# The half swap of a rotary embedding: from a TensorE product to four transfers within SBUF

## The chip, the cores and the metric

The kernel runs on one core of one Trainium2 chip. The metric is the device time of one execution in microseconds (us). TensorE does the matrix products, VectorE and ScalarE the elementwise work, GpSimd a few additions and small loads, and SyncE's queue starts the transfers of the weights. On the profile these are PE (with PEld for its weight loads), DVE, ACT, POOL and SP.

## The reference

Two blocks follow each other on 256 tokens of width 2048, all in float32. The first is a recurrent and banded-attention mixer with a feed-forward part. The second puts 16 learned tokens in front and mixes with two kinds of attention; one of them (heads "a") normalises its queries and keys and then turns them by angles that belong to the token's row and column in a grid:

```
def rope_half(x, ang):
    x1, x2 = jnp.split(x, 2, axis=-1)
    c, s = jnp.cos(ang), jnp.sin(ang)
    return jnp.concatenate([x1 * c - x2 * s, x2 * c + x1 * s], axis=-1)

def axial_rope(x, ang_row, ang_col):
    xr, xc = jnp.split(xf, 2, axis=-1)
    return jnp.concatenate([rope_half(xr, ang_row), rope_half(xc, ang_col)], axis=-1)

    q = axial_rope(rmsnorm(heads_first(qa, A_HEADS, HEAD_DIM), q_g), ang_row, ang_col)
    k = axial_rope(rmsnorm(heads_first(ka, A_KV_HEADS, HEAD_DIM), k_g), ang_row, ang_col)
```

A head has 128 columns: 64 for the row angle and 64 for the column angle, and each 64 are two halves of 32. Turning needs, for every half, the other half of its pair: the "half swap". There are 2 key heads on 272 tokens and 8 query heads on 256.

## The kernel before

**Tiling.** Every weight matrix is read once, in chunks of 256 rows by 512 columns (512 KB). A chunk is loaded by SP into `raw`, rounded to a high part `whi` by ACT (`split_hi`, L899), and the remainder `wlo` is made by DVE (`split_lo`, L1301). TensorE multiplies each chunk in 24 matmuls (`chunk_t`, L446; three products for two halves and four column blocks). There are four slots of `raw`, `whi` and `wlo`. ACT and DVE work four chunks ahead (`LEAD`): at place k, that is behind chunk k, they make the parts of chunk k+4, and ACT's rounding waits until TensorE has finished chunk k (`pe_done`).

**The second mixer.** Its input projection has 13 groups of 8 chunks (`G_IN2`, `NC`), places 0 to 103 by `NC * j + k`. All attention work of this block is done between these chunks, on every engine by a written-out order: behind chunk k, each engine runs what its own list has for place k. No planner is at work; each engine's list is a Python loop, and semaphores join them. Of the list, these matter here:

- `values_turn` (L710 to L712) behind chunks 43 to 47 transposes value tiles, two of them at a place, into PSUM; ACT and DVE copy them out (`values_copy`, DVE L1651 and L1652) and free the PSUM bank for the tile four further on.
- The attention units of heads "b" lie behind chunks 49 to 68: `scores` (L748), `weights_turn` (L771), `values` (L781). `values(u)` writes the one PSUM bank 7 and so waits until DVE has copied unit u-1 out of it (`unit_out`, L1758, semaphore `u_o`), and until ACT has copied the transposed weights (`unit_copy`, L1199, semaphore `u_pt`).
- `b_norm` on DVE and `b_turn` (L802) on TensorE follow at places 70 to 77; at place 78 TensorE waits until ACT (L1220) and DVE (L1780) have copied both turned halves (`bn_copied`) before three transposes at L509.
- The units of heads "a" begin at place 79.

**The rotary step** runs three times, n = 0 (keys, 2 tiles of 272 columns), 1 and 2 (queries, 4 tiles of 256), from places 41, 65 and 74 (`ROPE_FROM`). The raw head is in `qg`. ACT squares it into `qsq` and scales `qg` by the gain (semaphore `nr_ev`, two counts). One place after another then come:

- TensorE, place `first`: `rope_squares`, a product of `qsq` with ones (L722), into a PSUM set.
- ACT, place `first + 1`: `rope_root`, Ln and Exp for the reciprocal root (L1174, L1176), each behind a load of its function table.
- TensorE, place `first + 3`: `rope_turn_halves`, a product of `qg` with the constant `turn` (L732; the swap with its signs), into the same PSUM set.
- DVE, place `first + 4`: `rope` step 0, that product times the sine into `qrot` (L1664), which also frees the PSUM set (`set_free`); then steps 1 to 3 at the places of `ROPE_STEPS`: `qg` times the cosine (L1666), the sum (L1669), times the reciprocal root (L1672).

`turn` is loaded at the start by POOL among eight small constants (`N_CONST`). ACT starts no transfer in this kernel; SP and POOL do. `qg`, `qsq` and `qrot` lie in one large region of SBUF whose tiles stand at fixed distances from its beginning; the region begins behind the named tiles, `turn` among them.

The functions that the change touches:

Of the kernel before, what the change touches and what calls it, by code (L numbers as in the profile page):

```python
# [15 lines left out]
P = 128  # L16
# [64 lines left out]
POS_A = (31, *range(33, 40), *range(41, 48), 49)  # L81

LAMBDA_INIT = 0.8 - 0.6 * math.exp(-0.3 * 0)
N_CONST = 8
N_VEC = 8
VEC_ROWS = 68

# [24 lines left out]
def program(nc, x, w_in, lb_logits, hg_norm_w, rel_bias, w_branch_a, w_branch_b, w_out, norm_mix_w,  # L112
            norm_mlp_w, w_up, w_down, norm_final_w, meta_tokens_2, pre_norm_g_2, w_in_2, q_norm_g_2,
            k_norm_g_2, lambda_q1_2, lambda_k1_2, lambda_q2_2, lambda_k2_2, subln_g_2, w_out_2,
            post_norm_g_2, identity, level_masks, rope_cos, rope_sin, rope_turn, distance, rel_turned, triangles, out):
    with ExitStack() as ctx:
        def sb(name, shape, dt=F32):
            return ctx.enter_context(nc.sbuf_tensor(name, shape, dt))

        def sem(name):  # L120
            return ctx.enter_context(nc.semaphore(name))
# [32 lines left out]
        rs_b, ss_b, rn_b = [b_sums[:, i, :] for i in range(3)]  # L154
        cos_t = sb("cos_t", [P, TM])
        sin_t = sb("sin_t", [P, TM])
        turn = sb("turn", [P, P])
        dist = sb("dist", [P, NT, TM])
        ps = ctx.enter_context(nc.psum_tensor("ps", [P, 8, 512], F32))

        def at(name, kib, shape, dt=F32):
# [124 lines left out]
        br_m, br_hi, br_ready = sem("br_m"), sem("br_hi"), sem("br_ready")  # L286
        up_sq, up_hi, up_ready = [sem(n) for n in ("up_sq", "up_hi", "up_ready")]
        vt_t, vt_c = [sem("vt_t0"), sem("vt_t1")], [sem("vt_c0"), sem("vt_c1")]
        nr_ev, nr_ss, nr_sd, nr_rs, nr_rot, nr_done = [sem(n) for n in (
            "nr_ev", "nr_ss", "nr_sd", "nr_rs", "nr_rot", "nr_done")]  # L290
        u_s, u_nm, u_exp, u_p, u_t, u_pt, u_pv, u_o = [sem(n) for n in (
            "u_s", "u_nm", "u_exp", "u_p", "u_t", "u_pt", "u_pv", "u_o")]
        bn_ss, bn_ms, bn_sd, bn_n, bn_t, bn_y, bn_hi, yb2_ready = [sem(n) for n in (
# [16 lines left out]
        def pset(s):  # L310

            return ps[:, 2 * s:2 * s + 2, :].rearrange("p b (x c) -> p (b x) c", x=2)
# [115 lines left out]
        def _(pe):  # L428
# [293 lines left out]
                    ins = mm(ps[:, 2 * s + i, 0:w], ones[:], src, start=True, stop=True)  # L722
                ins.then_inc(nr_ss, 1)

            def rope_turn_halves(n, s):

                pe.wait_ge(nr_sd, n + 1)
                pe.wait_ge(nr_ev, 2 * n + 2)
                for i in range(2):
                    src = qg[:, i, :] if n == 0 else qg[:, 2 * i:2 * i + 2, 0:T]  # L730
                    w = TM if n == 0 else 2 * T
                    ins = mm(ps[:, 2 * s + i, 0:w], turn[:], src, start=True, stop=True)  # L732
                ins.then_inc(nr_rot, 1)

            def scores(u):
                hd, t = divmod(u % B_UNITS, NT)
                if u == 0:
# [90 lines left out]
            for j in range(G_IN2):  # L828
                c0 = C_IN2 + NC * j
                kv = j < 5  # L830
                if kv:
                    pe.wait_ge(set_free[j % 2], SETS_BEFORE_2 + j // 2)
                    if j == 0:
                        pe.wait_ge(x_ready, 2 * KT + 12)
                    elif j == 1:
                        pe.wait_ge(r_ready, 1)
                    else:
                        pe.wait_ge(kvb_free[j % 2], j // 2)
                    outs = [ps[:, b + i, 0:TM] for b in kv_banks(j) for i in range(2)]
                else:  # L840
                    s = set_of(j)
                    pe.wait_ge(set_free[s], need2[j])
                    outs = blocks(s)
                for k in range(NC):
                    if j == 0:
                        if k == 2:
                            turn_group(2, 3, down_free[3])
                        pe.wait_ge(x_ready, 2 * KT + CK * (k + 1))
                        if k == NC - 1:
                            pe.wait_ge(r_diag, NT)  # L850
                            pe.wait_ge(x_ready, 3 * KT)
                            for t in range(NT):
                                ins = mm(ps[:, 6, t * P:(t + 1) * P], ones[:], diag[:, t, :], start=True, stop=True)
                            ins.then_inc(r_mm, 1)
                    if j == 5:
                        pe.wait_ge(hi_packed, CK * k + CK - 1)
                        pe.wait_ge(lo_packed, CK * k + CK)
                    xh, xl = (None, xw_lo) if kv else (uhi, ulo)
                    chunk_t(c0, k, CK * k, xh, xl, outs, TM if kv else T, k == 0, k == NC - 1, shared=not kv)
                    if j == 5 and k >= 3:  # L860
                        values_turn(2 * (k - 3))
                        values_turn(2 * (k - 3) + 1)
                    for n, first in enumerate(ROPE_FROM):
                        if NC * j + k == first:
                            rope_squares(n, ROPE_SETS[n])
                        if NC * j + k == first + 3:
                            rope_turn_halves(n, ROPE_SETS[n])
                    if j >= J_B:
                        side(NC * (j - J_B) + k)

# [20 lines left out]
        def _(act):  # L891
# [276 lines left out]
            def rope_root(n, s):  # L1168
                act.wait_ge(nr_ss, n + 1)
                if n == 0:  # L1170
                    dst, src = qsq[:, 0:2, :], ps[:, 2 * s:2 * s + 2, 0:TM]
                else:
                    dst, src = qsq[:, :, 0:T], pset(s)
                f(dst, src, ACT.Ln, bias=eps_t[:], scale=1.0 / P).then_inc(nr_sd, 1)  # L1174
                act.wait_ge(nr_sd, n + 1)
                f(dst, dst, ACT.Exp, scale=-0.5).then_inc(nr_rs, 1)  # L1176

            def unit_exp(u):
                act.wait_ge(u_nm, u + 1)
# [48 lines left out]
            for j in range(G_IN2):  # L1228
                for k in range(NC):
# [23 lines left out]
                        side(NC * (j - J_B) + k)  # L1253
                    for n, first in enumerate(ROPE_FROM):
                        if NC * j + k == first + 1:
                            rope_root(n, ROPE_SETS[n])
                    if j == G_IN2 - 1 and k in (1, 3):
                        y_upper(1, k // 2, ob, bn_y, bn_hi)
# [29 lines left out]
        def _(dve):  # L1288
# [362 lines left out]
                nc.vector.tensor_copy(v_nat[:, b, :, :], ps[:, 4 + b % 4, 0:T].rearrange("p (t c) -> p t c", t=2))  # L1651
                nc.vector.tensor_copy(v_meta[0:META, b, :], ps[0:META, 4 + b % 4, T:T + P]).then_inc(vt_c[0], 1)  # L1652

            rope_free = (SETS_BEFORE_2 + 4, need2[7] + 1, need2[8] + 1)

            def rope(n, step):
                s = ROPE_SETS[n]
                w = TM if n == 0 else T
                nb = 2 if n == 0 else 4
                v, r, q = qg[:, 0:nb, 0:w], qrot[:, 0:nb, 0:w], qsq[:, 0:nb, 0:w]  # L1660
                if step == 0:
                    dve.wait_ge(nr_rot, n + 1)
                    src = ps[:, 2 * s:2 * s + 2, 0:TM] if n == 0 else pset(s)
                    tt(r, src, spread(sin_t[:], [0, nb], [1, w]), ALU.mult).then_inc(set_free[s], 1)  # L1664
                if step == 1:
                    own(tt(v, v, spread(cos_t[:], [0, nb], [1, w]), ALU.mult))  # L1666
                if step == 2:
                    dve.wait_ge(set_free[s], rope_free[n])
                    own(tt(v, v, r, ALU.add))  # L1669
                if step == 3:  # L1670
                    dve.wait_ge(nr_rs, n + 1)
# [189 lines left out]
        def _(pool):  # L1861
# [10 lines left out]
            for row, src, n in vectors:  # L1872
# [1 line left out]
            small = [  # L1874
                (lamv[:, 0], row_all(lambda_q1_2, DH)), (lamv[:, 1], row_all(lambda_k1_2, DH)),
                (lamv[:, 2], row_all(lambda_q2_2, DH)), (lamv[:, 3], row_all(lambda_k2_2, DH)),
                (cos_t[:], rope_cos), (sin_t[:], rope_sin), (turn[:], rope_turn),
                (dist[:], distance.rearrange("(t p) k -> p t k", p=P)),
            ]
            assert len(small) == N_CONST  # L1880
# [114 lines left out]
def shape_constants():  # L1995
# [17 lines left out]
    half = np.concatenate([ang[0], ang[0], ang[1], ang[1]], axis=1).T  # L2013
    rope_cos, rope_sin = np.cos(half).astype(f32), np.sin(half).astype(f32)

    turn = np.zeros((P, P), f32)
    for m in range(P):
        if (m // 32) % 2 == 0:
            turn[m + 32, m] = -1.0
        else:  # L2020
            turn[m - 32, m] = 1.0
    qpos = places + META
    kpos = np.concatenate([places + META, np.arange(META)])
    distance = np.abs(qpos[:, None] - kpos[None, :]).astype(f32)
    return {"identity": identity, "level_masks": masks, "rope_cos": rope_cos, "rope_sin": rope_sin,
            "rope_turn": turn, "distance": distance}, {"triangles": triangles}


# [19 lines left out]
```

## Time and profile before

| | us |
|---|---|
| median of 3 runs | 1893.94 |
| the 3 runs | 1893.53, 1894.71, 1893.94 |
| span of the profiled execution | 1893.3 |
| PE busy in it | 1879.6 |
| DVE busy | 1101.4 |
| ACT busy | 889.3 |
| POOL busy | 143.6 |

The span goes from the first to the last instruction of one profiled execution; no other time of that execution is recorded, and the median of the runs stands 0.6 us above its span. Matmuls are pipelined: the start of one to the start of the next tells its cost, not its duration. The granted clock of TensorE is 0.999 over the span.

### The profile page before, as it was taken

The numbers are of one execution on the slowest core, as the hardware profiler recorded it, in microseconds if no ns is written. First come the engines' busy times: TensorE is split into PE (matmuls) and PEld (weight loads), VectorE is DVE, ScalarE is ACT, GpSimd is POOL, SyncE is SP. The second block draws the span as 40 slices with busy tenths as digits, with TensorE's granted clock in tenths as the row PEclk, the third lists the DMA queues.
The fourth block names the chain that finished last, engine by engine and source line by source line (L and its number), as shares of the span: only waits on it lengthen the run. The fifth ranks groups of instructions, "written<-read, shape, count | busy, mean of one in ns | idle before, by whom it ended". The sixth has DMA issues, their size and how long they took to land.

```text
span 1893.3 us, 33876 instructions
## 1 busy us (share of the span) xinstructions
PE 1879.6 (99%) x13432; PEld 1743.7 (92%) x13432; DVE 1101.4 (58%) x1270; ACT 889.3 (47%) x1171; POOL 143.6 (8%) x122
## 2 busy tenths in 40 slices
PE   9999999999999999999999999999999999999998
PEld 9989998999999889988998899899889999899986
DVE  6556766667655555545445445445565556767664
ACT  6544444455544445443444344334454355664543
POOL 2001322411001100000010000000010000000000
PEclk9999999999999999999999999999999999999999
DMA  8566565566565656656665665566556655354454
GB/s 270 184 181 177 181 179 178 165 200 180 168 231 191 214 186 179 194 198 192 196 192 193 194 191 194 194 190 190 189 185 181 179 170 150 105 147 144 156 190 143
DMA packets 176434, 346.47 MB, mean 183 GB/s; under 512 B 10976, under 2 KB 11184, under 8 KB 175776
## 3 DMA queue, kind: packets, MB, share of 16 engines
q1 hardware_dynamic: 174176, 337.76, 57.2%
q0 software_dynamic: 2128, 6.82, 1.4%
q8 instruction: 101, 1.65, 0.4%
q14 instruction: 29, 0.24, 0.0%
HBM read 342.44 MB, written 2.10 MB: 182 GB/s over the span
## 4 chain that ended last, share of the span: by engine, by line
PE 97%; DVE 1%; ACT 0%; DMA 0%; issue 0%; SPq 0%; DVEq 0%; ACTq 0%
PE ps L446 58%; PE ps L458 33%; PE ps L548 1%; PE ps L781 1%; DVE wlo L1301 1%; PE ps L771 1%; PE ps L748 1%; PE ps L791 0%; DMA raw<-in_w_in_dram 0%; ACT whi L899 0%; PE ps L476 0%; PE ps L759 0%; PE ps L599 0%; PE ps L591 0%; DVE xlo L1323 0%; PE ps L610 0%
## 5 line engine op out<-in xcount | busy, mean ns | idle before, releaser
L1301 DVE TENSOR_TENSOR wlo<-raw,whi 128x1024 fp32r<-128x1024 f32 x631 | 796.5, 1268 | 698.1 <-ACT whi L899 697.1
L899 ACT ACTIVATE whi<-raw 128x1024 fp32r<-128x1024 f32 x631 | 664.5, 1058 | 886.3 <-PE ps L446 551.5
L446 PE MATMUL ps<-xhi,whi 128*128 128x256 f32 (+1 forms) x1904 | 542.2, 285 | 0.4 <-DVE wlo L1301 0.3
L446 PE MATMUL ps<-xhi,wlo 128*128 128x256 f32 (+1 forms) x1904 | 531.3, 279 | 0.0
L446 PE MATMUL ps<-xlo,whi 128*128 128x256 f32 x1664 | 462.5, 278 | 0.0
L446 PEld LDWEIGHTS ps<-xhi,whi 128*128 128x128 f32 x1904 | 359.1, 189 | 9.3 <-issue 6.7
L446 PEld LDWEIGHTS ps<-xhi,wlo 128*128 128x128 f32 x1904 | 357.8, 188 | 0.0
L446 PEld LDWEIGHTS ps<-xlo,whi 128*128 128x128 f32 x1664 | 313.4, 188 | 1.5 <-issue 0.7
L446 PE MATMUL ps<-x2hi,whi 128*128 128x256 f32 x1024 | 282.8, 276 | 0.0
L446 PE MATMUL ps<-x2hi,wlo 128*128 128x256 f32 x1024 | 282.7, 276 | 0.0
L446 PE MATMUL ps<-x2lo,whi 128*128 128x256 f32 x1024 | 282.7, 276 | 0.0
L446 PEld LDWEIGHTS ps<-x2lo,whi 128*128 128x128 f32 x1024 | 192.2, 188 | 0.2
L446 PEld LDWEIGHTS ps<-x2hi,whi 128*128 128x128 f32 x1024 | 192.2, 188 | 0.2
L446 PEld LDWEIGHTS ps<-x2hi,wlo 128*128 128x128 f32 x1024 | 192.2, 188 | 0.0
L458 PE MATMUL ps<-whi,ya_lo 128*128 128x512 f32 x256 | 100.8, 394 | 0.0
L458 PE MATMUL ps<-whi,yb_lo 128*128 128x512 f32 x256 | 100.8, 394 | 0.0
L458 PE MATMUL ps<-whi,xlo 128*128 128x512 f32 x256 | 100.8, 394 | 0.0
L458 PE MATMUL ps<-wlo,ya_hi 128*128 128x512 f32 x256 | 100.3, 392 | 0.0
L458 PE MATMUL ps<-wlo,yb_hi 128*128 128x512 f32 x256 | 100.2, 392 | 0.0
L458 PE MATMUL ps<-whi,xhi 128*128 128x512 f32 x256 | 100.2, 391 | 0.0
L458 PE MATMUL ps<-wlo,xhi 128*128 128x512 f32 x256 | 100.1, 391 | 0.0
L458 PE MATMUL ps<-whi,ya_hi 128*128 128x512 f32 x256 | 99.7, 390 | 0.0
(373 smaller groups left out, 2370.6 us busy)
## 6 DMA issues: line engine op xcount, KB each, us to landing
raw<-in_w_in_dram SPq DMA_DIRECT2D x279, 512.0 KB, 3.8
raw<-in_w_up_dram SPq DMA_DIRECT2D x128, 512.0 KB, 3.7
raw<-in_w_down_dram SPq DMA_DIRECT2D x128, 512.0 KB, 3.7
raw<-in_w_out_dram SPq DMA_DIRECT2D x64, 512.0 KB, 3.8
raw<-in_w_branch_a_dram SPq DMA_DIRECT2D x16, 512.0 KB, 4.9
raw<-in_w_branch_b_dram SPq DMA_DIRECT2D x16, 512.0 KB, 3.8
x_nat<-in_x_dram SPq DMA_DIRECT2D x4, 512.0 KB, 7.4
rel<-in_rel_turned_dram POOLq DMA_DIRECT2D x8, 256.0 KB, 4.3
```

Of the source, the lines that this page charges most:

```text
L446: ins = mm(outs[b], w[:, k % SLOTS, j, cols], v, start=start, stop=last and j == CK - 1 and i == 2, skip_group_check=True)
L458: ins = mm(ps[:, 2 * s + t, :], v[:, kt, toks], w[:, k % SLOTS, j, :], start=first and j == 0 and i == 0, stop=last and j == CK - 1 and i ...
L548: ins = mm(misc[:, hd // 4, (hd % 4) * P:(hd % 4 + 1) * P], k_both[:, hd, :], spread(qp[:, hd, 0:1], *both_tiles), start=True, stop=True)
L748: ins = mm(ps[:, 4 + i, 0:TM], qb[f, hd, t * P:(t + 1) * P], kb[f, hd, :], start=True, stop=True)
L771: ins = nc.tensor.transpose(ps[:, 6, i * P:(i + 1) * P], p[:, i * P:(i + 1) * P], ident[:])
L781: ins = mm(ps[:, 7, 0:P], pt2[:, u % 2, i * P:(i + 1) * P], v, start=i == 0, stop=i == 2)
L899: f(whi[:, k % SLOTS], raw[:, k % SLOTS], ACT.Copy).then_inc(whi_ready, 1)
L1301: tt(wlo[:, k % SLOTS], raw[:, k % SLOTS], whi[:, k % SLOTS], ALU.subtract).then_inc(wlo_ready, 1)
```

## The change

The product with `turn` is taken out, with the constant, its load and its tile. In its place ACT starts four transfers from `qg` to `qrot`, each of which moves a block of 32 partitions onto its neighbour block; the sign is in the sine constant. ACT does this at place `first + 1`, ahead of `rope_root`. Step 0 on DVE waits for the four transfers (semaphore `nr_rot`, 16 counts each) and multiplies in place, from SBUF. The PSUM set is freed by ACT, right behind its Ln.

```
             def rope_squares(n, s):
                 ...
-            def rope_turn_halves(n, s):
-
-                pe.wait_ge(nr_sd, n + 1)
-                pe.wait_ge(nr_ev, 2 * n + 2)
-                for i in range(2):
-                    src = qg[:, i, :] if n == 0 else qg[:, 2 * i:2 * i + 2, 0:T]
-                    w = TM if n == 0 else 2 * T
-                    ins = mm(ps[:, 2 * s + i, 0:w], turn[:], src, start=True, stop=True)
-                ins.then_inc(nr_rot, 1)
...
-                        if NC * j + k == first + 3:
-                            rope_turn_halves(n, ROPE_SETS[n])
...
                 f(dst, src, ACT.Ln, bias=eps_t[:], scale=1.0 / P).then_inc(nr_sd, 1)
                 act.wait_ge(nr_sd, n + 1)
+                act.sem_inc(set_free[s], 1)
                 f(dst, dst, ACT.Exp, scale=-0.5).then_inc(nr_rs, 1)
+
+            def rope_swap(n):
+
+                act.wait_ge(nr_ev, 2 * n + 2)
+                if n:
+                    act.wait_ge(nr_done, n)
+                for b in range(4):
+                    to, of = slice(32 * b, 32 * b + 32), slice(32 * (b ^ 1), 32 * (b ^ 1) + 32)
+                    v = (slice(0, 2), slice(0, TM)) if n == 0 else (slice(0, 4), slice(0, T))
+                    act.dma_start(qrot[to, v[0], v[1]], qg[of, v[0], v[1]]).then_inc(nr_rot, 16)
...
                         if NC * j + k == first + 1:
+                            rope_swap(n)
                             rope_root(n, ROPE_SETS[n])
...
                 if step == 0:
-                    dve.wait_ge(nr_rot, n + 1)
-                    src = ps[:, 2 * s:2 * s + 2, 0:TM] if n == 0 else pset(s)
-                    tt(r, src, spread(sin_t[:], [0, nb], [1, w]), ALU.mult).then_inc(set_free[s], 1)
+                    dve.wait_ge(nr_rot, 64 * (n + 1))
+                    tt(r, r, spread(sin_t[:], [0, nb], [1, w]), ALU.mult).then_inc(nr_sin, 1)
...
                 if step == 2:
-                    dve.wait_ge(set_free[s], rope_free[n])
+                    dve.wait_ge(nr_sin, n + 1)
                     own(tt(v, v, r, ALU.add))
...
-                (cos_t[:], rope_cos), (sin_t[:], rope_sin), (turn[:], rope_turn),
+                (cos_t[:], rope_cos), (sin_t[:], rope_sin),
...
+    first_halves = (np.arange(P) // 32) % 2 == 0
+    rope_sin[first_halves] = -rope_sin[first_halves]
```

## Rows read from the trace of the kernel before

**Rows 1.** The page: busy time of each engine, and the final chain by engine.
```profile
PE 1879.6 (99%) x13432; PEld 1743.7 (92%) x13432; DVE 1101.4 (58%) x1270; ACT 889.3 (47%) x1171; POOL 143.6 (8%) x122
...
PE 97%; DVE 1%; ACT 0%; DMA 0%; issue 0%; SPq 0%; DVEq 0%; ACTq 0%
```

**Rows 2.** The chain in order of time, second mixer: start us, us, what.
```profile
1566.89 0.92 PE ps L732 x4
...
1665.31 2.83 PE ps L446 x24
1668.14 1.72 PE ps L732 x4
...
1670.90 16.35 PE ps L446 x144
...
1699.02 1.72 PE ps L732 x4
```

**Rows 3.** Timeline of PE: start us, us, engine, line, operation, out<-in, count.
```profile
1570.48 0.27 PE L710 MATMUL ps<-ident,v_t 128*128 128x128 f32 x1
...
1669.70 0.65 PE L781 MATMUL ps<-v_nat,pt 128*128 128x128 f32 x4
...
1703.32 0.49 PE L509 MATMUL ps<-ident,kb 128*128 128x128 f32 x3
```

**Rows 4.** Timeline of DVE around the three steps; in brackets the idle time before.
```profile
1566.15 2.50 DVE L1301 TENSOR_TENSOR wlo<-raw,whi 128x1024 fp32r<-128x1024 f32 x2 [3.72 <-ACT whi L899]
...
1568.90 0.27 DVE L1652 COPY v_meta<-ps 16x128 f32<-16x128 f32 x1
...
1669.23 0.28 DVE L1758 COPY o_nat<-ps 128x128 f32<-128x128 f32 x1
...
1701.57 0.74 DVE L1780 TENSOR_SCALAR ob<-ps,subg 128x512 f32<-128x512 f32 x1
...
1705.81 1.22 DVE L1664 TENSOR_TENSOR qrot<-ps,sin_t 128x1024 f32<-128x1024 f32 x1
...
1727.61 1.22 DVE L1666 TENSOR_TENSOR qg<-qg,cos_t 128x1024 f32<-128x1024 f32 x1
```

**Rows 5.** Timeline of ACT around places 42, 66 and 75.
```profile
1560.11 1.06 ACT L899 ACTIVATE whi<-raw 128x1024 fp32r<-128x1024 f32 x1 [2.47 <-PE ps L446]
1561.18 1.28 ACT L1174 ACT_TABLE_LOAD   x1
...
1566.34 1.06 ACT L899 ACTIVATE whi<-raw 128x1024 fp32r<-128x1024 f32 x1 [0.22 <-PE ps L446]
...
1660.58 1.06 ACT L899 ACTIVATE whi<-raw 128x1024 fp32r<-128x1024 f32 x1 [0.69 <-PE ps L446]
1661.55 0.47 ACT L1199 ACTIVATE pt<-ps 128x384 f32<-128x384 f32 x1
...
1662.33 1.28 ACT L1174 ACT_TABLE_LOAD   x1
...
1667.01 1.05 ACT L899 ACTIVATE whi<-raw 128x1024 fp32r<-128x1024 f32 x1
...
1691.80 1.06 ACT L899 ACTIVATE whi<-raw 128x1024 fp32r<-128x1024 f32 x1 [1.39 <-PE ps L446]
1692.88 1.28 ACT L1174 ACT_TABLE_LOAD   x1
```

**Rows 6.** SP's queue at the start, issues back to back: start us, us.
```profile
0.76 0.40 SPq L377 DMA_DIRECT2D ident<-in_identity_dram  x1
1.21 0.42 SPq L378 DMA_DIRECT2D mix_rows<-in_norm_mix_w_dram  x1
...
4.12 0.69 SPq L381 DMA_DIRECT2D x_nat<-in_x_dram  x1
```

**Rows 7.** Transfers by line: count, KB each, median us from issue to landing.
```profile
raw<-in_w_in_dram SPq DMA_DIRECT2D x279, 512.0 KB, 3.8
```

**Rows 8.** Waits of PEld from 1540 us on: total us, times, longest.
```profile
PEld ps L446 <- DVE qrot L1664: 0.5, 1, 0.5
```

More of the change, by code:

```diff
@@ L83 @@
 LAMBDA_INIT = 0.8 - 0.6 * math.exp(-0.3 * 0)
-N_CONST = 8
+N_CONST = 7
 N_VEC = 8
@@ L114, in program @@
             k_norm_g_2, lambda_q1_2, lambda_k1_2, lambda_q2_2, lambda_k2_2, subln_g_2, w_out_2,
-            post_norm_g_2, identity, level_masks, rope_cos, rope_sin, rope_turn, distance, rel_turned, triangles, out):
+            post_norm_g_2, identity, level_masks, rope_cos, rope_sin, distance, rel_turned, triangles, out):
     with ExitStack() as ctx:
@@ L156, in program @@
         sin_t = sb("sin_t", [P, TM])
-        turn = sb("turn", [P, P])
         dist = sb("dist", [P, NT, TM])
@@ L288, in program @@
         vt_t, vt_c = [sem("vt_t0"), sem("vt_t1")], [sem("vt_c0"), sem("vt_c1")]
-        nr_ev, nr_ss, nr_sd, nr_rs, nr_rot, nr_done = [sem(n) for n in (
-            "nr_ev", "nr_ss", "nr_sd", "nr_rs", "nr_rot", "nr_done")]
+        nr_ev, nr_ss, nr_sd, nr_rs, nr_rot, nr_sin, nr_done = [sem(n) for n in (
+            "nr_ev", "nr_ss", "nr_sd", "nr_rs", "nr_rot", "nr_sin", "nr_done")]
         u_s, u_nm, u_exp, u_p, u_t, u_pt, u_pv, u_o = [sem(n) for n in (
@@ L1652, in values_copy @@
                 nc.vector.tensor_copy(v_meta[0:META, b, :], ps[0:META, 4 + b % 4, T:T + P]).then_inc(vt_c[0], 1)
-            rope_free = (SETS_BEFORE_2 + 4, need2[7] + 1, need2[8] + 1)
             def rope(n, step):
-                s = ROPE_SETS[n]
                 w = TM if n == 0 else T
@@ L2014, in shape_constants @@
     rope_cos, rope_sin = np.cos(half).astype(f32), np.sin(half).astype(f32)
[L2016 to L2021, printed above, removed]
+    first_halves = (np.arange(P) // 32) % 2 == 0
+    rope_sin[first_halves] = -rope_sin[first_halves]
     qpos = places + META
@@ L2025, in shape_constants @@
     return {"identity": identity, "level_masks": masks, "rope_cos": rope_cos, "rope_sin": rope_sin,
-            "rope_turn": turn, "distance": distance}, {"triangles": triangles}
+            "distance": distance}, {"triangles": triangles}
 def kernel(**inputs):
```

## The prediction

> **What bounds the kernel now.** I read the page first, then the chain, then the stretch of the change engine by engine. On the page [rows 1] the reader is to see that TensorE is busy for 99% of the span and makes 97% of the chain that ended last: whatever leaves its queue for good comes off the time, as long as it doesn't have to wait there for something else. So the question is not what the products cost but what TensorE meets when it arrives earlier. In the chain [rows 2] the three products with `turn` stand as pieces of their own, between chunks; in TensorE's timeline [rows 3] I then looked for the first instruction behind each product that waits for another engine, and in the timelines of DVE and ACT [rows 4, 5] for when that other engine was done. ACT is the engine that gets new work, and in just this stretch it is the one that runs late: the Ln and Exp of each rotary step, with a table load of 1.28 us before each, push its rounding of weights back.
>
> **What is removed.** The products cost TensorE 0.92 + 1.72 + 1.72 = 4.36 us [rows 2]. That is 0.23% of the time, and a difference of about 0.2% (3.8 us) is what a measurement of this kernel can tell from no change. Almost all of it would have to come back to count.
>
> **What is added on ACT.** Each swap is four issues. ACT starts no transfer in this trace; the nearest rows are SP's at the start of the kernel, back to back [rows 6]: 0.40 us busy and 0.45 us from one to the next, at most 0.69 us (0.74 with the 0.05 us between two) when large transfers are queued. I take 0.45, since a swap moves 68 KB or 128 KB per transfer and SP issues one only every chunk, and keep 0.74 as the upper bound: 1.8 us per swap, at most 3.0. While ACT's queue issues, it hands out nothing that stands behind: the table load, Ln, Exp, the rounding of the next chunk, and then a copy for TensorE. What ACT has already begun goes on, so part of the 1.8 us is hidden by it:
>
> - n = 0: the rounding of place 42 starts at 1560.11; the four issues run from about 1560.2 to 1562.0 beside it, the table load that came at 1561.18 comes at 1562.0: late by 0.8 us [rows 5].
> - n = 1: at place 66 the rounding starts at 1660.58, but the copy behind it waits for TensorE until 1661.55, and issues that stand behind an unmet wait can't begin. From about 1661.7 to 1663.5; the table load came at 1662.33: late by 1.2 us.
> - n = 2: like n = 0, from 1691.9 to 1693.7 against 1692.88: late by 0.8 us.
>
> If nothing is hidden the delay is 1.8 us each; if an issue costs ACT next to nothing it is zero. Both ends stay in the range. The two waits of `rope_swap` (for ACT's own scaling of `qg` and for the step before) are long met.
>
> **What TensorE meets, step by step.**
>
> - n = 0. Behind chunk 45 the transposes at L710 start at 1570.48 [rows 3]; without the product TensorE is there at 1570.48 - 0.92 = 1569.6. They need DVE's copies of place 44, whose last one ends at 1568.90 + 0.27 = 1569.17 [rows 4]. So today there are 0.4 us to spare. DVE's two weight parts ahead of it waited 3.72 us for ACT's rounding, so ACT's delay goes through, less the 0.22 us for which ACT stood idle at 1566.34 [rows 5]: copies at 1569.8, TensorE at 1569.9. Gain 0.6 us, and 0.92 if ACT loses nothing.
> - n = 1. Behind chunk 68 `values(15)` waits until DVE has copied unit 14 out of the one PSUM bank. That copy runs from 1669.23 to 1669.51 [rows 4], right behind a `wlo` that waits for ACT's rounding of 1667.01, which stands directly behind the late Exp [rows 5]. TensorE started `values(15)` at 1669.70 [rows 3]. So this product, 1.72 us from 1667.98, hid a wait that is there without it: what comes back is 1669.70 - 1669.6 = 0.1 us, and ACT's delay of 1.2 us goes onto the path whole. Loss 1.1 us.
> - n = 2. Behind chunk 78 TensorE's L509 waits for both halves of `bn_copied`; it started at 1703.32 [rows 3], and without the product it is there at 1701.6. DVE's second copy, again behind ACT's roundings, ends at 1701.57 + 0.74 = 1702.31 [rows 4]. At most 0.95 us come back, less ACT's 0.8: gain 0.2 us.
>
> Sum: 0.6 - 1.1 + 0.2 = -0.3 us, a small loss.
>
> **Smaller parts.** The PSUM set of n = 2 is freed by ACT some 10 us earlier, which takes away one wait of 0.5 us at chunk 80 [rows 8]; I don't count it, because the units of heads "a" that begin there hang on DVE and ACT, whose work is timed from the end of chunk 79, and TensorE would wait for them 0.5 us longer. It goes to the lower bound. Step 0 on DVE reads SBUF instead of PSUM: 1.22 us in both forms (L1664 and L1666 [rows 4]), nothing. The load of `turn` and its wait lie far ahead of their use. The tile of 512 bytes per partition is gone, so the large region moves down by that much; no row shows that an address matters, and I count nothing. TensorE's matmuls run at one of two paces: the 144 behind place 68 take 16.35 us, 113.5 ns each, the 24 of chunk 68 take 2.83 us, 117.9 ns each [rows 2]. Which one a stretch gets changes with what stands before it, and the product before the 144 goes away. At the slower pace they cost 144 x 4.4 ns = 0.6 us more. I put in half, 0.3 us, as I can't tell.
>
> **The transfers.** The four are begun together and step 0 on DVE takes them three places later: for n = 2 issues end at 1693.7 and step 0 stands at 1705.81 [rows 4], and even 1.4 us earlier than that leaves some 10.7 us, the least of the three. A weight chunk of 512 KB lands in 3.8 us [rows 7], and the four together are 272 KB or 512 KB. Nothing is queued behind them on ACT's transfers; on DVE the next weight part stands behind step 0. Weight loads that share the engines with them have about three chunks, over 8 us, in hand. So the landing is hidden, with 6 us to spare.
>
> **The numbers.** Forecast: 0.3 + 0.3 = 0.6 us lost, which is no change that can be measured. The span of 1893.3 becomes 1893.9, and with the 0.6 us by which the median stands above it 1894.5 us. Low end: ACT loses nothing and the wait of rows 8 counts, 0.92 + 0.1 + 0.95 + 0.5 = 2.5 us gained, 1891.5. High end at 0.45 us an issue with nothing hidden: -0.4 - 1.7 - 0.85 = -2.95, with the slow pace -3.6: 1897.5.
>
> **The rivals.**
>
> *All 4.4 us come back.* For it: the chain is TensorE from end to end and shows no wait at these places [rows 1, 2]. The time would be 1893.9 - 4.4 = 1889.6, or 1889.1 with the wait of rows 8. Against it: at L781 DVE's copy ends 0.2 us before TensorE starts, so the trace hides the wait only because the product lay over it. It would take an earlier ACT, and nothing moves ACT forward. 0.05, with all that I can't see on this side.
>
> *The issues are nearly free to ACT.* 1891.5 to 1892.5, no measurable change either. For it: the sequencer that issues is not the part that computes. Against it: 0.40 us busy on SP's queue for every one [rows 6], in an engine that hands out its instructions in order. 0.13. The Trainium skill says the same thing as this rival (DMA: Bandwidth & Descriptors, section "Issuing engines are not separate DMA queues"): beginning transfers on several engines saves the time to initiate them, usually small beside the transfer. By that rule the sum would be a gain of 2.5 us; by the row it is a loss of 0.3, and no run here shows yet what an issue costs on ACT.
>
> *The issues are dear, so the kernel is slower.* The place is n = 1, where ACT's delay is TensorE's. With d the delay at each swap and the gains above, every 0.1 us more per issue costs 0.4 us three times, 1.2 us. From the -0.6 forecast, the loss passes 3.8 us when an issue takes 0.45 + 3.2 / 12 = 0.72 us, just under the dearest row of SP [rows 6]; with nothing hidden as well, from 0.47 us on. At 0.74 us it is 1898.0, and with nothing hidden 1901. For it: ACT is no SP, and SP issues weights at the same time. Against it: short transfers cost 0.45. 0.13.
>
> *The transfers land late.* If the four ran one after another, each like a weight load, they would need 4 x 3.8 = 15.2 us [rows 7] against 10.7: DVE would stand 4.5 us at step 0 with the next weight part behind it, and TensorE would lose most of this in the attention units of n = 2 and some at the other two, 1899 to 1904. Against it: the weight loads too overlap one another. 0.03. The Trainium skill speaks for this case (same page, "Rules for kernel authors"): transfers to disjoint parts of the partitions serialize, and one over all 128 is to be preferred. Its formula on that page (section "Anatomy of one DMA", for transfers that GpSimd starts), 2.0 us plus bytes over 436 GB/s, gives as an estimate 4 x 2.3 = 9.2 us if each also waited out the one before, still inside the 10.7; no run here shows it yet.
>
> **Chances.** The forecast's case (ACT late by 0.5 to 1.8 us a swap, 1893 to 1897.5) has 0.66. Faster by over 0.2%: 0.05. Within 0.2%: 0.66 + 0.13 + a little of the dear issues = 0.81. Slower: 0.14. The range is 1891.7 to 1898.0; it leaves out the first rival, a late landing and the worst of the dear issues.
>
> **What would show it.** In the changed kernel: four issues on ACT's queue before each of the three first table loads, 0.4 to 0.5 us each; the table loads late by about 0.8, 1.2 and 0.8 us against TensorE's end of the chunk before; a wait of TensorE of 2.5 to 3 us ahead of L781 behind chunk 68, for DVE's L1758; one of about 1.5 us ahead of L509 behind chunk 78 and of 0.3 us ahead of L710 behind chunk 45; no wait of DVE for the transfers at step 0. I am wrong if ACT's table loads come no later, if DVE waits at L1664's place, if the granted clock falls behind the wait at chunk 68, or if chunks far from the second mixer change their pace.

## The result and the profile after

Six runs of the changed kernel take 1899.71 to 1902.4 us, median 1900.03; six of the kernel before 1892.09 to 1895.63, median 1893.74. The ratio is 1.0034, with a 95% interval of 1.0022 to 1.0045: slower by 6.3 us, 2 us beyond the upper end of the range. The forecast of 1894.5, no measurable change, was wrong.

Of the page after, the lines that answer to [rows 1]: busy time of each engine, and the chain that ended last, by engine.

```profile
PE 1876.0 (99%) x13420; PEld 1741.8 (92%) x13420; DVE 1101.9 (58%) x1270; ACT 889.1 (47%) x1171; POOL 143.1 (8%) x121
...
PE 95%; DVE 2%; ACT 1%; issue 1%; DMA 0%; ACTq 0%; SPq 0%; DVEq 0%
```

TensorE has 12 products fewer and is 3.6 us less busy, in a span of 1898.1 us that is 4.8 us longer. Its share of the chain went from 97% to 95%; DVE, ACT and "issue" gained what it lost. So TensorE now waits.

Where, the waits of PEld from 1540 us on tell (line waited for and what ended the wait: total us, times, longest):

```profile
PEld ps L770 <- issue: 4.8, 2, 4.1
PEld ps L508 <- issue: 2.8, 1, 2.8
...
PEld ps L709 <- DVE v_meta L1651: 1.3, 1, 1.3
```

These are the places that the prediction named: L770 is `values(15)` behind chunk 68 (L781 before), L508 the transposes behind chunk 78 (L509), L709 those behind chunk 45 (L710). The wait of [rows 8] is gone, as expected. "issue" hides the releaser here; PE's own timeline shows it in brackets:

```profile
1569.20 0.33 PE L709 MATMUL ps<-ident,v_t 128*128 128x128 f32 x1 [1.09 <-DVE v_meta L1651]
...
1670.84 1.19 PE L770 MATMUL ps<-v_nat,pt 128*128 128x128 f32 x4 [3.92 <-DVE o_nat L1753]
...
1707.89 0.52 PE L508 MATMUL ps<-ident,kb 128*128 128x128 f32 x3 [2.61 <-DVE ob L1775]
```

ACT's timeline at the three places, against [rows 5] (ACTq is the issue of transfers, in brackets the idle time before):

```profile
1558.60 1.06 ACT L886 ACTIVATE whi<-raw 128x1024 fp32r<-128x1024 f32 x1 [2.47 <-PE ps L445]
1558.62 2.55 ACTq L1174 DMA_DIRECT2D qrot<-qg  x4
1561.21 1.28 ACT L1161 ACT_TABLE_LOAD   x1 [1.55 <-issue]
...
1659.37 1.06 ACT L886 ACTIVATE whi<-raw 128x1024 fp32r<-128x1024 f32 x1 [0.69 <-PE ps L445]
1660.33 0.47 ACT L1197 ACTIVATE pt<-ps 128x384 f32<-128x384 f32 x1
1660.37 0.67 ACTq L1174 DMA_DIRECT2D qrot<-qg  x1
...
1661.38 1.99 ACTq L1174 DMA_DIRECT2D qrot<-qg  x3
1663.41 1.28 ACT L1161 ACT_TABLE_LOAD   x1 [2.32 <-issue]
...
1695.44 1.06 ACT L886 ACTIVATE whi<-raw 128x1024 fp32r<-128x1024 f32 x1 [1.38 <-PE ps L445]
1695.52 2.65 ACTq L1174 DMA_DIRECT2D qrot<-qg  x4
1698.20 1.28 ACT L1161 ACT_TABLE_LOAD   x1 [1.70 <-issue]
```

From the start of the rounding to the start of the table load it is 2.61, 4.04 and 2.76 us, where [rows 5] have 1.07, 1.75 and 1.08. ACT is late by 1.5, 2.3 and 1.7 us; forecast were 0.8, 1.2 and 0.8. The issues do run beside work that ACT has begun, but four take 2.6 us and not 1.8, and at n = 1 they take 3.0, because 0.34 us pass there between the end of the first and the start of the second.

How ACT's delay reaches TensorE at n = 1, DVE's timeline shows: the weight part waits for ACT's late rounding, and the copy of unit 14, for which `values(15)` waits, stands right behind it.

```profile
1669.27 1.23 DVE L1300 TENSOR_TENSOR wlo<-raw,whi 128x1024 fp32r<-128x1024 f32 x1 [6.53 <-ACT whi L886]
1670.41 0.28 DVE L1753 COPY o_nat<-ps 128x128 f32<-128x128 f32 x1
```

Last, something that the sum did not hold. Behind the 3.92 us wait the matmuls of the next chunk start 213 ns apart until 1676.09, where others are 113 to 118 apart. The stretches (us; busy time and count of PE, PEld, DVE, ACT, POOL; granted clock; DMA share; GB/s), first after:

```profile
1667.00:1669.00 2.00, 0.00 (x0) 0.00 (x0) 0.00 (x0) 1.99 (x3) 0.00 (x0) 1.00 0.00 0
1669.00:1671.00 2.00, 0.16 (x1) 0.19 (x2) 1.54 (x3) 2.00 (x7) 0.00 (x0) 0.56 0.00 0
1671.00:1676.00 5.00, 5.00 (x24) 5.00 (x25) 1.40 (x2) 0.14 (x2) 0.00 (x0) 0.50 0.72 202
1676.00:1681.00 5.00, 5.00 (x46) 5.00 (x46) 2.36 (x2) 2.25 (x4) 0.00 (x0) 0.99 0.08 18
```

and before, the same five microseconds, behind the same place:

```profile
1671.00:1676.00 5.00, 5.00 (x47) 5.00 (x46) 1.28 (x3) 1.35 (x3) 0.00 (x0) 1.00 0.65 205
```

TensorE is fully busy in both, but does 24 matmuls in place of 47: the granted clock is 0.50, the level of 1.2 GHz instead of 2.4.

**The account.** The start of the same TensorE instruction, after less before, tells what each stretch lost:

| | after - before, us | lost since the row above |
|---|---|---|
| first sum-of-squares product, n = 0 | 1554.60 - 1556.11 = -1.51 | |
| behind chunk 45 | 1569.20 - 1570.48 = -1.28 | 0.23 |
| behind chunk 68 (`values(15)`) | 1670.84 - 1669.70 = 1.14 | 2.42 |
| sum-of-squares product, n = 2 | 1690.72 - 1687.09 = 3.63 | 2.49, the half clock |
| behind chunk 78 | 1707.89 - 1703.32 = 4.57 | 0.94 |
| end of the span | 1898.1 - 1893.3 = 4.8 | 0.2 |

The loss is 6.3 us from the first row on. The 1.51 us by which this execution is ahead at the first row have nothing to do with the change: the same 1.51 us lie between the two executions 61 us after the start already, and such leads and lags appear in every run below. It is rather the execution before that was late. In the later runs a time stands 1.7 to 2.9 us above the span of the same execution, 1.8 at the median, so the 0.6 us between the median before and the profiled span mean that the execution before took some 1.2 us more than its median (an estimate from these figures). I therefore compare kernels by the **stretch** from the first sum-of-squares product of n = 0 to the end of the span: 337.2 us before, 343.5 after.

### The profile page after: what moved, and what is told of

Same layout as the page of the kernel before. It is cut to its first block, busy times and chain, and to the rows that moved or that the text cites. A ratio compares the mean times of both kernels' runs of the same rounds, so it can differ in the third digit from the quotient of the medians.

```text
span 1898.1 us, 33865 instructions
## 1 busy us (share of the span) xinstructions
PE 1876.0 (99%) x13420; PEld 1741.8 (92%) x13420; DVE 1101.9 (58%) x1270; ACT 889.1 (47%) x1171; POOL 143.1 (8%) x121
## 4 chain that ended last, share of the span: by engine, by line
PE 95%; DVE 2%; ACT 1%; issue 1%; DMA 0%; ACTq 0%; SPq 0%; DVEq 0%
PE ps L445 57%; PE ps L457 32%; DVE wlo L1300 1%; PE ps L547 1%; ACT whi L886 1%; PE ps L770 1%; PE ps L737 1%; PE ps L760 1%; PE ps L780 0%; DMA raw<-in_w_in_dram 0%; PE ps L475 0%; ACTq L1174 0%; PE ps L748 0%; PE ps L598 0%; PE ps L590 0%
```

## The experiments

My theory after the result: an issue costs ACT 0.65 us and not 0.45; the delay passes to TensorE whole at n = 1, because `values(15)` waits there for work that stands behind ACT's table loads; and the long wait brings half clock, which costs 2.5 us more. Rivals: the address of the large region, the transfers' bytes, the landing, a loss that is even over the three swaps, and half clock that costs nothing in the end because TensorE would wait anyway. The results together:

| kernel | median us (before, same chip) | ratio, 95% interval | first row, span, stretch us |
|---|---|---|---|
| SP begins all swaps | 1892.49 (1894.3) | 0.9993, 0.9984 to 1.0003 | 1553.84, 1889.3, 335.5 |
| filler of two products | 1899.94 (1894.3) | 1.003, 1.0019 to 1.0042 | 1557.08, 1898.0, 340.9 |
| two issues per swap | 1894.76 (1894.3) | 1.0001, 0.9992 to 1.0011 | 1554.31, 1892.4, 338.1 |
| address restored | 1901.05 (1894.3) | 1.0035, 1.0023 to 1.0048 | 1556.53, 1900.7, 344.2 |
| SP begins n = 1 alone | 1895.92 (1893.66) | 1.0009, 1.0 to 1.0018 | 1556.64, 1897.6, 341.0 |
| filler of four products | 1899.14 (1893.66) | 1.0023, 1.0014 to 1.0032 | 1556.44, 1899.4, 343.0 |
| later root at n = 1 | 1895.62 (1893.66) | 1.0006, 0.9997 to 1.0015 | 1555.40, 1892.8, 337.4 |
| SP, later root at n = 1 | 1890.68 (1893.66) | 0.9983, 0.9974 to 0.9992 | 1554.32, 1888.8, 334.5 |
| one issue per swap | 1893.85 (1894.84) | 0.9992, 0.9982 to 1.0001 | 1557.02, 1894.5, 337.4 |
| SP, later roots at n = 1, 2 | 1894.77 (1894.84) | 0.9999, 0.999 to 1.0008 | 1554.79, 1891.5, 336.7 |

**SP begins the transfers.** The same 12 transfers, from another queue.

```
 # SP, between its loads, which run ahead of the other engines
+if NC * j + k == first + 9:
+    rope_swap(n)          # as in the changed kernel, with sp. in place of act.
 # ACT, place first + 1
-    rope_swap(n)
     rope_root(n, ROPE_SETS[n])
```

> The same twelve transfers, but begun by SP's queue at the same places. Theory (the four issues hold ACT's list for 2.6 us a swap, TensorE waits for what ACT hands out late, and behind the long wait at chunk 68 its clock falls): ACT is as early as in the kernel before, TensorE waits 1.6 to 1.8 us ahead of the L781 work behind chunk 68 and some 0.8 us ahead of the three transposes behind chunk 78, the clock stays full, and the time is 1891.5 to 1893 us, about 2 us under the kernel before. Rival one (the transfers themselves cost, by landing late or by slowing the weight loads): still 1897 us or more. Rival two (the shift of the large SBUF region by 512 bytes): still 1900 us.

1892.49 us; the loss is gone. TensorE behind chunk 68, and the swap's issues on SP (duration in ns, least, median, most):

```profile
1666.37 0.68 PE L783 MATMUL ps<-v_nat,pt 128*128 128x128 f32 x4 [1.60 <-DVE o_nat L1755]
```
```profile
L384 SPq DMA_DIRECT2D qrot<-qg x12: 572/599/894, 1560.6 to 1694.7; - x12
```

Two readings. `values(15)` still waits 1.60 us, nearly the 1.72 us of the product that stood there: the product hid a wait, as the prediction said. And an issue of this transfer costs SP 0.60 us, like ACT's 0.62. It is not ACT that is dear but this transfer: SP's own weight loads in the changed kernel (512 KB out of DRAM) take 0.37 us to issue.

```profile
L371 SPq DMA_DIRECT2D raw<-in_w_in_dram x279: 367/372/537, 3.6 to 1775.2; - x140
...
L1174 ACTq DMA_DIRECT2D qrot<-qg x12: 604/624/691, 1558.6 to 1697.5; - x12
```

**Two issues in place of four.** Each moves 64 partitions; halves of the wrong pairs are exchanged, so the rotary step computes something else.

```
-for b in range(4):
-    to, of = slice(32 * b, 32 * b + 32), slice(32 * (b ^ 1), 32 * (b ^ 1) + 32)
+for b in range(2):
+    to, of = slice(64 * b, 64 * b + 64), slice(64 * (b ^ 1), 64 * (b ^ 1) + 64)
...
-    dve.wait_ge(nr_rot, 64 * (n + 1))
+    dve.wait_ge(nr_rot, 32 * (n + 1))
```

> Two transfers of 64 partitions in place of four of 32, begun by ACT at the same places: the same bytes move, but not the right halves, so the swap itself is left out. Theory: ACT's list is held for 1.3 us instead of 2.6 if an issue costs the same whatever it moves; the table loads are late by about 0.3, 1.1 and 0.4 us, TensorE waits some 2.8 us at chunk 68, the clock stays full: 1893 to 1895 us. If an issue costs by its rows (twice as many): 2.6 us again and 1899 to 1901 us. Rival one: the same bytes, so 1899 us or more.

**One issue.** One transfer over 128 partitions, which exchanges nothing; the rotary step again computes something else.

```
-for b in range(4):
-    ...
-    act.dma_start(qrot[to, v[0], v[1]], qg[of, v[0], v[1]]).then_inc(nr_rot, 16)
+act.dma_start(qrot[:, v[0], v[1]], qg[:, v[0], v[1]]).then_inc(nr_rot, 16)
...
-    dve.wait_ge(nr_rot, 64 * (n + 1))
+    dve.wait_ge(nr_rot, 16 * (n + 1))
```

> ScalarE begins one transfer over all 128 partitions per swap in place of four over 32; it moves the same bytes but exchanges no halves, so the rotary step computes something else. Theory (an issue costs ScalarE some 0.63 us whatever it moves: 0.62 over 32 partitions, 0.64 over 64): one issue of 0.6 to 0.7 us, which lies beside the rounding that already runs, so no table load is late by over 0.3 us, no fall of the clock, the stretch from the first sum-of-squares product of n = 0 to the end as with SyncE's issues, 335.5 us (up to 336.1 at the slower pace), and about 1892.5 us in all. Rival (the price goes with partitions or bytes): an issue of over 1.2 us, table loads late by 0.5 us or more, 338 us in the stretch, as with two transfers, and over 1894.5 in all.

The bytes of a swap are the same in all three. With two issues, then with one (ns):

```profile
L1174 ACTq DMA_DIRECT2D qrot<-qg x6: 548/638/657, 1558.3 to 1692.0; - x6
```
```profile
L1172 ACTq DMA_DIRECT2D qrot<-qg x3: 547/652/655, 1561.0 to 1693.6; - x3
```

0.62, 0.64, 0.65 us over 32, 64 and 128 partitions: for these transfers the price is one per issue, whatever part of the swap it moves. The stretch follows: 343.5 with four, 338.1 with two, 337.4 with one, 335.5 with none on ACT. The last step was expected to be nothing: with one issue I had written 335.5 to 336.1 and a full clock. ACT's table load at n = 1 does come when it came before (1.75 us behind the rounding), but the wait behind chunk 68 is 1.94 us, 0.34 longer than with SP's issues, and a short stretch of half clock follows it (18 matmuls in 3.3 us):

```profile
1669.80 0.99 PE L770 MATMUL ps<-v_nat,pt 128*128 128x128 f32 x4 [1.94 <-DVE o_nat L1751]
```
```profile
1670.10:1673.40 3.30, 3.30 (x18) 3.30 (x17) 1.26 (x2) 0.00 (x1) 0.00 (x0) 0.50 0.66 182
```

That part of the expectation failed. ACT is late in another place here: it stands idle for 0.42 us between Ln and the second table load, which it doesn't with SP's issues; why isn't shown. The two-issue kernel has such a stretch of half clock too, behind a wait of 2.23 us, where a full clock was expected; its time of 1894.76 us lies within the 1893 to 1895 expected.

**The address.** An unused tile of 512 bytes per partition where `turn` stood.

```
+sb("turn_place", [P, P])
```

> The changed kernel with an unused tile of 512 bytes where the constant of the product stood, so that every tile has its old address. Theory and rival one: 1899 to 1901 us as without it. Rival two (addresses): back to 1894 us.

1901.05 us, as slow as the change, with the same wait of 3.92 us behind chunk 68 and the same half clock. The address isn't what the loss comes from; this rival is out.

**SP begins the swap of n = 1 alone.** ACT keeps n = 0 and n = 2.

```
 # SP: as above, for n = 1 alone
...
 # ACT, place first + 1
-    rope_swap(n)
+    if n != 1:
+        rope_swap(n)
```

> Only the swap of n = 1 is begun by SyncE, those of n = 0 and n = 2 stay with ScalarE. I compare by the stretch from the first sum-of-squares product of n = 0 to the end of the span, 343.5 us in the changed kernel, 337.2 in the kernel before, 335.5 with all three swaps on SyncE. Theory (the swap of n = 1 carries nearly all: 2.36 us of a longer wait behind chunk 68 and 2.49 us of half clock behind that): no table load late at n = 1, no fall of the clock, 343.5 - 4.85 = 338.7 us, and about 1895.2 us in all; the wait ahead of the identity products behind chunk 78 stays. Rival (the loss is the same at each of the three swaps): a third of 343.5 - 335.5, so 340.8 us and about 1897.3 in all.

1895.92 us in all, nearer to my theory; but 341.0 us in the stretch, where the rival had 340.8. The profile says why it is longer than 338.7:

```profile
1705.83 0.52 PE L521 MATMUL ps<-ident,kb 128*128 128x128 f32 x3 [2.40 <-DVE ob L1789]
```
```profile
1671.00:1676.00 5.00, 5.00 (x46) 5.00 (x45) 1.21 (x3) 1.29 (x3) 0.00 (x0) 1.00 0.72 206
...
1706.60:1709.90 3.30, 3.30 (x17) 3.30 (x17) 1.35 (x2) 0.00 (x0) 0.00 (x0) 0.50 0.78 232
```

Behind chunk 68 the clock is full, as expected. But in this execution it fell behind chunk 78, where the wait of 2.40 us is no longer than the 2.61 us that had no such sequel after the change: chunk 79 takes 4.44 us there, 1.5 more than the 2.91 of the changed kernel. And the 144 matmuls behind place 68 run at the slower pace, 17.04 us, 0.6 more than at 114 ns each. 338.7 + 1.5 + 0.6 = 340.8. So this execution shows that n = 2's wait can cost a stretch of half clock too. It is the slowest of the eleven, 1899.96 us. Seven of them had a granted clock of 0.999, as the kernel before has in all 78 later executions; the median of the seven is 1895.42, where the theory had 1895.2 and the rival 1897.3. So n = 1 does carry what I gave it.

**Filling the wait.** Products that nobody reads, in the wait behind chunk 68, to keep TensorE at work (two in one kernel, four in the other).

```
+def fill(n, s):
+    pe.wait_ge(nr_sd, n + 1)
+    for i in range(2):      # range(4), with 2 * s + i % 2, in the second
+        mm(ps[:, 2 * s + i, 0:2 * T], ident[:], dist[:, :, 0:T], start=True, stop=True)
...
+if NC * j + k == first + 3 and n == 1:
+    fill(n, ROPE_SETS[n])
```

> The changed kernel, and behind chunk 68 alone TensorE is given 1.7 us of products again whose result nobody reads. Nothing on ACT or in the transfers is different. Theory: TensorE's wait at chunk 68 shrinks from 4.1 to about 2.4 us, its clock doesn't fall, and the 2.6 us that the half clock cost come back: 1897 to 1898 us. If the clock falls all the same, or is not part of the loss: 1900 us. Both rivals (transfers, addresses): 1900 us.

> As the run with two products of 128 x 512 put into the wait behind chunk 68, with four of them (they compute nothing that is used). Theory (the half clock behind the wait costs 2.5 us by itself): the clock stays full, the wait left behind the products is some 0.7 us, the stretch from the first sum-of-squares product of n = 0 is 340.9 us against 343.5 in the changed kernel, and the time about 1897.5, up to 1899.5 if the first 140 us run at the slower pace of the first such run. Rival (TensorE would have waited for those 2.5 us elsewhere anyway): the clock stays full and the stretch is 343.5 us all the same.

With two, then with four, the 5 us behind the wait:

```profile
1674.00:1679.00 5.00, 5.00 (x47) 5.00 (x46) 1.30 (x3) 1.35 (x3) 0.00 (x0) 1.00 0.71 212
```
```profile
1674.00:1679.00 5.00, 5.00 (x45) 5.00 (x44) 1.22 (x2) 1.35 (x3) 0.00 (x0) 1.00 0.64 203
...
1707.60:1710.90 3.30, 3.11 (x15) 3.14 (x16) 2.31 (x3) 0.00 (x0) 0.00 (x0) 0.50 0.85 259
```

Behind chunk 68 the clock is full in both; the tail of the wait behind the filler ends for the same DVE copy (2.21 and 0.48 us). With two products the stretch is 340.9 us, 2.6 less than in the changed kernel: that is the half clock, given back. With four it is 343.0: the clock fell behind chunk 78 instead, and the slow pace took 0.6 us.

The medians hardly show it, 1899.94 and 1899.14 us, 0.7 and 0.8 us less above their own runs of before than the changed kernel. The reason is on record: the clock falls in some executions of these kernels and not in others. Of the seven with two products three have a granted clock of 0.999 (the profiled one among them), 1898.54 us in the mean, and four have 0.998, 1900.66 us. Of the eleven with four products seven have 0.999, 1898.14 us, and four 0.998, 1900.98 us. The executions at full clock stand 3.9 us above the mean of their runs of before in both cases, where the changed kernel stands 6.7 above, also in the mean. So 2 to 3 us are the half clock, and TensorE does not lose them elsewhere when the clock stays full.

**The root one place later.** In place of removing ACT's issues, take away what stands between them and the copy: at n = 1, Ln and Exp with their table loads move behind the next copy for TensorE.

```
 # ACT
 if NC * j + k == first + 1:
     rope_swap(n)
+if NC * j + k == first + (2 if n == 1 else 1):
     rope_root(n, ROPE_SETS[n])
```

> ScalarE begins the swaps as in the changed kernel, but Ln and Exp of n = 1 (and their table loads) are queued one place later, behind the copy for which values(15) waits. Theory (the copy behind chunk 68 is late because it stands behind the issues and the table loads): values(15) doesn't wait, the clock stays full, and the 1.72 us of the product come back as well: 343.5 - 4.85 - 1.72 = 336.9 us in the stretch, about 1893.4 us in all. Rival (the issues alone hold the copy): a wait of over 1 us ahead of values(15), 338 us or more and over 1894.5 in all.

TensorE behind chunk 68 and behind chunk 78:

```profile
1667.54 0.61 PE L770 MATMUL ps<-v_nat,pt 128*128 128x128 f32 x4
...
1702.68 0.30 PE L508 MATMUL ps<-ident,kb 128*128 128x128 f32 x1 [2.33 <-DVE ob L1776]
```

No wait behind chunk 68 (no bracket), and 337.4 us in the stretch, 0.5 above what I expected, which the slow pace of the 144 accounts for. The median, 1895.62, is 2.2 us above 1893.4. Here too the granted clocks on record tell more: seven of the eleven executions have 0.998, 1896.13 us in the mean, and the four with 0.999, the profiled one among them, 1894.78, which is 0.5 us above the mean of the kernel before, as the stretch is 0.2 above. A wait of 2.33 us behind chunk 78 remains, about as long as in the two profiled executions whose clock fell there; that it fell there in the seven isn't shown.

**Both.** SP begins the swaps, and the root of n = 1 is one place later.

> Both: SyncE begins all three swaps, and Ln and Exp of n = 1 are queued one place later on ScalarE. Theory: the three products come back as 0.92 + 1.72 + 0.95 us, less what ScalarE needs at n = 0 and n = 2 anyway: 335.5 - 1.7 = 333.7 us in the stretch and about 1890.8 us in all, 3.5 us under the kernel before. Rival (DVE's first step of n = 1 then waits for the later root and TensorE for DVE): 335.5 us and 1892.5, as with SyncE alone.

1890.68 us, ratio 0.9983: faster than both kernels, 3.0 us below the one before and, each taken against its own runs of before, 9.3 below the changed one. The stretch is 334.5 us, 0.8 above the theory's 333.7, and 0.6 of that is the slow pace of the 144. Only one wait of the three is left, 0.71 us behind chunk 78:

```profile
1665.09 0.61 PE L783 MATMUL ps<-v_nat,pt 128*128 128x128 f32 x4
...
1698.61 0.52 PE L521 MATMUL ps<-ident,kb 128*128 128x128 f32 x3 [0.71 <-DVE ob L1777]
```

**The root of n = 2 later as well,** to take away those 0.7 us: `first + (2 if n else 1)`.

> As the run with SyncE's issues and the root of n = 1 one place later, with the root of n = 2 one place later too. Theory (the 0.7 us that TensorE still waits ahead of the identity products behind chunk 78 come from the two table loads at place 75): that wait goes, 334.5 - 0.7 = 333.8 us in the stretch, about 1890.0 us in all. Rival (the late rounding only meets TensorE or DVE one place on, at the first units of heads a): 334.5 us or more in the stretch, 1890.7 or more in all.

```profile
1701.33 0.41 PE L521 MATMUL ps<-ident,kb 128*128 128x128 f32 x2 [3.10 <-DVE ob L1777]
```

The rival, and at the same place: the wait grows to 3.10 us, the stretch to 336.7, the time to 1894.77. One place later the table loads stand ahead of the rounding for which DVE's weight part waits 4.52 us, and DVE's half of `bn_copied` stands behind that part. No granted clock below 1.00 follows this wait in the profiled execution; five of the eleven have 0.998.

## Why the prediction was wrong

**What bounds the kernel.** Right. All but 0.2 us of the loss is TensorE waiting, or running at half clock, at the places that the prediction named.

**What the product hid.** Right at all three places. With SP's issues, where ACT is not late, the stretch is 1.7 us shorter than before: the forecast for that case was 0.92 + 0.1 + 0.95 us, near enough.

**The price of an issue on ACT: the first step that failed.** "I take 0.45, since a swap moves 68 KB or 128 KB per transfer" read a price by bytes out of SP's first rows [rows 6]. It is 0.62 us, 0.65 from one to the next, the same for 32 and for 128 partitions, and 0.60 on SP for the same transfers, while DRAM loads of 512 KB cost SP 0.37. The nearest rows were of another kind of transfer. Four issues take 2.6 us, and 3.0 at n = 1, so ACT is late by 1.5, 2.3 and 1.7 us. Taking from each of the prediction's three terms what ACT is later than forecast gives 0.6 - 0.7, -1.1 - 1.1 and 0.2 - 0.9, in sum a loss of 3.0 us; the account has 0.23, 2.42 and 0.94, in sum 3.6. It goes the way of the rival of the dear issues, but stops short of the 0.72 us at which that rival had the kernel measurably slower: without what follows the time would have stayed within the range. What the price depends on (memory at the source, rows per partition) wasn't tried.

The prediction weighed this with the Trainium skill (DMA: Bandwidth & Descriptors, section "Issuing engines are not separate DMA queues"), by which the time to initiate is usually small beside the transfer. The trace agrees in proportion, 0.62 us against a landing of 5.0 us at the median, and it decides nothing here: nobody waits for the landing, and ACT's list waits for the issues. More to the point is Perfetto Trace Analysis of the same skill (section "DMA Instruction — HWDGE (DVE, Sync)"): the sequencer that issues is free for its next instruction at the end of the profiled window of an issue. The trace agrees: the last of the three issues ends at 1661.38 + 1.99 = 1663.37, and the table load starts at 1663.41.

**The granted clock: the second step that failed, a term that was missing.** The sum held TensorE at full clock through a wait that it put at 2.5 to 3 us, and named the clock only among what would make it wrong. It fell, for 6.8 us, and cost 2.49. Of the 6.3 us lost, 3.6 are ACT's delay (0.23 + 2.42 + 0.94), 2.5 the clock, and 0.2 come after chunk 78. In the profiled executions SP's issues and the later root, which shorten the wait or remove it, leave the clock full behind chunk 68, and the filler does so while TensorE still can't go on. That the half clock comes with these waits and costs about 2 us is shown; which waits have such a sequel is not (below).

**The smaller parts.** The wait of [rows 8] went and was lost again at the first units of heads "a", as forecast: 4.57 us behind chunk 78, 4.8 at the end. No run shows the 0.3 us for the pace as a cost of the change: behind place 68, outside the half clock, both kernels run at 113 ns. In six of the later kernels the same 144 matmuls run at the slow pace, 0.6 us, the upper bound given. The prediction let the pace hang on what stands before a stretch. In the trace before it does change only where other work stands between two stretches of chunk matmuls (some 40 times; within a stretch, once). But the same work doesn't give the same pace: behind `values(15)` and a wait of 1.60 us the 144 take 16.42 us with all of SP's swaps and 17.04 with that of n = 1 alone. Address and DVE's step 0 are nothing, as said.

**The landing.** Right. After the change no step 0 waits for the transfers; from issue to landing, with four, then with two and one per swap (count, KB each, median us):

```profile
qrot<-qg ACTq DMA_DIRECT2D x8, 128.0 KB, 5.0
...
qrot<-qg ACTq DMA_DIRECT2D x4, 68.0 KB, 3.9
```
```profile
qrot<-qg ACTq DMA_DIRECT2D x4, 256.0 KB, 5.7
```
```profile
qrot<-qg ACTq DMA_DIRECT2D x2, 512.0 KB, 5.1
```

The Trainium skill's warning against transfers to disjoint partitions (DMA: Bandwidth & Descriptors, section "Rules for kernel authors") holds in that four gain nothing over one: 5.0 us after its issue against 5.1. As four in a row, 15 us, they don't appear: the longest of the twelve lands after 6.4 us, and at n = 2, from the first issue to the last landing, four take 8.4 us and one 6.6. What the rule's advice would save is three issues of 0.65 us per swap: between four and one the stretch differs by 6.1 us. But one transfer over all partitions doesn't exchange halves.

## What to carry to other kernels

Price a transfer by the number of its issues on the queue that begins it, from rows of the same kind of transfer; on an engine that is late, each issue is a delay of everything behind it, and a queue with time to spare (SP here) does the same transfers without a loss that the stretch shows. Before taking work off TensorE, look for the wait that it covers, and move what causes that wait (here two table loads, one place later) in the same step. A new wait of some microseconds on TensorE may bring half clock, in some executions and not in others: keep that cost as a term of the sum, or at least as a rival with a chance. Compare kernels by a local stretch when a run can start a microsecond or two early or late, and look at the granted clock of every execution before taking one profile for all.

## What the runs showed that I had not expected

- **Waits and the clock.** In the profiled executions, waits of 3.92 (twice), 2.40, 2.34, 2.23 and 1.94 us were followed by half clock; waits of 3.10, 2.61, 2.57, 2.35, 2.33, 2.21 and 1.60 us (twice) were not. The granted clocks of all executions say the same of one and the same kernel:

  | kernel | longest wait behind chunks 68 and 78, us | executions at 0.999, mean us | executions below, mean us |
  |---|---|---|---|
  | before (78 later runs) | none | 78 | 0 |
  | SP, later root at n = 1 | 0.71 | 11, 1891.10 | 0 |
  | SP begins all swaps | 1.60 | 10, 1892.70 | 0 |
  | one issue per swap | 1.94 | 8, 1893.40 | 2, 1896.04 |
  | two issues per swap | 2.23 | 5, 1893.52 | 5, 1895.71 |
  | later root at n = 1 | 2.33 | 4, 1894.78 | 7, 1896.13 |
  | filler of four products | 2.34 | 7, 1898.14 | 4, 1900.98 |
  | SP begins n = 1 alone | 2.40 | 7, 1895.75 | 4, 1897.55 |
  | filler of two products | 2.57 | 3, 1898.54 | 4, 1900.66 |
  | SP, later roots at n = 1, 2 | 3.10 | 6, 1893.69 | 5, 1895.97 |
  | changed, and address restored | 3.92 | 0 | 12 |

  Within a kernel the executions with the lower clock are 1.4 to 2.8 us longer in the mean. In these kernels no execution fell with waits up to 1.60 us, every one with 3.92, and between them some did and some didn't, with no order by length. What decides there stays open, and for executions without a kept trace so does the place of the fall.
- **The pace far from the change.** At the first row the executions lie between 1553.84 and 1557.08 us, with nothing changed ahead of it for TensorE. In part that is the pace of matmuls: between 62 and 100 us the changed kernel's execution starts 338 and the first filler's 328, both fully busy at full clock (PE's count in these stretches, the changed kernel first):

```profile
62.00:100.00 38.00, 38.00 (x338) 38.00 (x337) 21.99 (x23) 16.47 (x18) 0.00 (x0) 1.00 0.65 201
```
```profile
62.00:100.00 38.00, 38.00 (x328) 37.97 (x327) 21.11 (x23) 16.30 (x17) 0.00 (x0) 1.00 0.63 191
```

  Ten matmuls of 0.114 us are 1.1 us in 38. What sets the pace was not found; it is as large as most effects here, so a median of a few runs tells 2 us only just.
